# Attention scores of paired heads: from 64 contracted rows to all 128, with each head's keys in a half-zero tile

## The reference, cut to what matters

```python
# ret, 5 heads, chunks of 128 tokens
intra = jnp.einsum('bnihd,bnjhd->bnhij', qc, kc).astype(f32) * decay_in
# moba, 5 heads
s_own = (jnp.einsum('bhqd,bhkd->bhqk', qc, k_own).astype(f32) * scale
         - slopes[:, None, None] * (q_pos[:, None] - own_pos[None, :]).astype(f32))
# mla, 6 heads, 64 + 32 dimensions
s = (jnp.einsum('bqhd,bkhd->bhqk', qn, k_nope)
     + jnp.einsum('bqhd,bkd->bhqk', qp, k_pe)).astype(jnp.float32) * scale
# dilated, 8 heads
scores = jnp.einsum('bnqrhe,bnkrhe->bnrhqk', qb.astype(F32), kb.astype(F32)) * (e ** -0.5)
```

## Time and profile before

| | |
|---|---|
| time, median of 3 executions | 2071.74 us (2069.88 to 2073.74) |
| the profiled execution, its own time | 2070.45 us |
| its span, first to last instruction | 2068.7 us |
| mean granted TensorE clock | 0.987 of 2.4 GHz |
| PE busy | 2012.9 us (97%), 9640 matmul passes |
| DVE busy, ACT busy | 1511.9 us (73%), 1239.2 us (60%) |
| attention steps of layer 0, of layer 1, dilated | about 50 to 125 us, 378 to 455 us, 1690 to 1746 us |

### The profile page before, as it was taken

One profiled execution on the slowest core, in us unless ns is written; L12 is line 12 of the kernel. 1 busy time (PEld: TensorE's weight loads), 2 busy tenths in 40 slices (PEclk: granted clock), 3 DMA queues, 4 the chain that ended last, 5 costly groups with the idle time before them and its releaser, 6 DMA issues.

```text
span 2068.7 us, 26452 instructions
## 1 busy us (share of the span) xinstructions
PE 2012.9 (97%) x9640; PEld 1677.9 (81%) x9640; DVE 1511.9 (73%) x1530; ACT 1239.2 (60%) x1298; POOL 98.5 (5%) x93
## 2 busy tenths in 40 slices
PE   7999999997999999999999999999899999999998
PEld 6878887886888888888888888878688888898887
DVE  6675446667999999989988998999754556565544
ACT  5544344545777777777777777777544455445443
POOL 0000000001000000000000000060010030000000
PEclk9989999998999999999999999999999999999999
DMA  8337554335999999999999999999655443435550
GB/s 336 119 128 273 182 181 156 133 109 222 380 378 383 376 383 376 381 374 383 380 379 372 383 385 368 370 407 364 220 183 188 161 168 143 163 118 198 183 185 38
DMA packets 78919, 548.73 MB, mean 265 GB/s; under 512 B 9008, under 2 KB 9136, under 8 KB 17280
## 3 DMA queue, kind: packets, MB, share of 16 engines
q1 hardware_dynamic: 73872, 522.98, 67.0%
q0 software_dynamic: 4960, 24.56, 3.2%
HBM read 540.68 MB, written 10.49 MB: 266 GB/s over the span
## 4 chain that ended last, share of the span: by engine, by line
PE 91%; DVE 5%; ACT 2%; issue 1%; DMA 0%; DVEq 0%; SPq 0%; ACTq 0%
PE ps L536 28%; PE ps L538 28%; PE ps L537 28%; DVE wlo L1843 2%; PE ps L812 1%; ACT whi L1386 1%; PE ps L709 1%; PE ps L1100 0%; PE ps L1121 0%; PE ps L1128 0%; PE ps L1002 0%; PE ps L982 0%; DMA bc<-in_rows 0%; DVE r L1923 0%; PE ps L1117 0%
## 5 line engine op out<-in xcount | busy, mean ns | idle before, releaser
L1843 DVE TENSOR_TENSOR wlo<-raw,whi 128x2048 fp32r<-128x2048 f32 (+4 forms) x506 | 1147.3, 2271 | 314.5 <-ACT whi L1386 307.7
L1386 ACT ACTIVATE whi<-raw 128x2048 fp32r<-128x2048 f32 (+4 forms) x506 | 950.4, 1879 | 201.1 <-PE ps L538 192.0
L536 PE MATMUL ps<-whi,xth 128*128 128x512 f32 (+3 forms) x1872 | 746.4, 399 | 8.6 <-DVE xtl L1881 3.8
L538 PE MATMUL ps<-whi,xtl 128*128 128x512 f32 (+3 forms) x1872 | 726.0, 388 | 0.0
L537 PE MATMUL ps<-wlo,xth 128*128 128x512 f32 (+3 forms) x1872 | 724.8, 387 | 0.0
L536 PEld LDWEIGHTS ps<-whi,xth 128*128 128x128 f32 x1872 | 354.8, 190 | 79.7 <-issue 8.0
L538 PEld LDWEIGHTS ps<-whi,xtl 128*128 128x128 f32 x1872 | 354.2, 189 | 70.5
L537 PEld LDWEIGHTS ps<-wlo,xth 128*128 128x128 f32 x1872 | 355.4, 190 | 63.1
L536 PE MATMUL ps<-whi,hth 128*128 128x512 f32 (+2 forms) x736 | 287.3, 390 | 2.1 <-DVE htl L2110 1.0
L538 PE MATMUL ps<-whi,htl 128*128 128x512 f32 (+2 forms) x736 | 285.4, 388 | 0.0
L537 PE MATMUL ps<-wlo,hth 128*128 128x512 f32 (+2 forms) x736 | 284.6, 387 | 0.0
(11 more groups left out here) (344 smaller groups left out, 1258.7 us busy)
## 6 DMA issues: line engine op xcount, KB each, us to landing
raw<-in_stream SPq DMA_DIRECT2D x475, 1024.0 KB, 5.8
raw<-in_stream SPq DMA_DIRECT2D x16, 768.0 KB, 4.3
bc<-in_rows POOLq DMA_DIRECT2D x4, 1024.0 KB, 4.9
slot_rows<-in_blank POOLq DMA_DIRECT2D x7, 512.0 KB, 9.5
kc<-slot_rows POOLq DMA_DIRECT2D x7, 512.0 KB, 7.6
sum_rows<-r POOLq DMA_DIRECT2D x7, 512.0 KB, 5.7
raw<-in_stream SPq DMA_DIRECT2D x4, 832.0 KB, 8.3
raw<-in_stream SPq DMA_DIRECT2D x4, 640.0 KB, 3.8
```

The source lines that it names most:

```text
L536: pe.matmul(o, ah, bh, start=start, stop=False, skip_group_check=True)
L538: return pe.matmul(o, al, bh, start=False, stop=stop, skip_group_check=True)
L1386: act.activation(whi[:, c.split, 0:c.width], raw[:, c.raw, 0:c.width], ACT.Copy).then_inc(hi_done, 1)
L1843: dve.tensor_tensor(wlo[:, c.split, 0:c.width], raw[:, c.raw, 0:c.width], f32(whi[:, c.split, 0:c.width]), ALU.subtract).then_inc(lo_done, 1)
```

## The change

Each head of a pair gets a key tile of its own with all 128 rows. They lie in columns 384 to 511 of `prob` (for the first head of a pair) and `probt` (for the second), 2 x 128 columns each. DVE sets the 64 rows that belong to the other head to zero, once, at the start of the program. ACT's one copy of a pair's queries and keys becomes three: the queries of both heads (128 rows x 256), the first head's keys (64 x 256) and the second head's keys (64 x 256). Since these key tiles have one buffer each and not two, the first key copy waits until the scores of head i-2 are done (semaphore `s` at i-1), the second for those of head i-1. `scores` contracts all 128 rows: the queries of both heads against the keys of one, so the other head's queries meet zeros. `mla` heads are left as they are.

```diff
+        lone_keys = [tile[:, :, 3 * P:4 * P] for tile in (prob, probt)]
...
                 def scores(n):
-                    rows = slice(HD * (n % 2), HD * (n % 2) + HD)
-                    q, k = qkt[rows, n // 2 % 2, 0:S], qkt[rows, n // 2 % 2, S:2 * S]
+                    q, k = qkt[:, n // 2 % 2, 0:S], lone_keys[n % 2]
...
                 def scores(i):
                     kind, n = WORK[i]
                     u = UNIT_OF[i]
-                    rows = slice(0, QD) if kind == "mla" else slice(HD * PAIR_OF[WORK[i]][1], HD * PAIR_OF[WORK[i]][1] + HD)
-                    q, k = qkt[rows, u % 2, 0:S], qkt[rows, u % 2, S:2 * S]
+                    rows = slice(0, QD if kind == "mla" else P)
+                    q, k = qkt[rows, u % 2, 0:S], qkt[rows, u % 2, S:2 * S].rearrange("p (t s) -> p t s", t=T)
+                    if kind != "mla":
+                        k = lone_keys[PAIR_OF[WORK[i]][1]]
                     o = ps[B_S]
                     pe.wait_ge(*at(hd, "qk", u + 1))
                     if i == 0:
                         pe.wait_ge(sem(f"kv{l}"), 1)
+                        pe.wait_ge(sem("blank_keys"), 2)
...
+            def take_pair(stage, i, buf):
+
+                act.activation(qkt[:, buf, 0:S], ps[B_TQ][:, 0:S], ACT.Copy)
+                for slot in range(2):
+                    rows = slice(HD * slot, HD * slot + HD)
+                    if i > 0:
+                        act.wait_ge(*at(stage, "s", i - 1 + slot))
+                    m = act.activation(lone_keys[slot][rows], ps[B_TQ][rows, S:2 * S].rearrange("p (t s) -> p t s", t=T), ACT.Copy)
+                m.then_inc(sem("qk"), 1)
...
-                    act.activation(qkt[:, i // 2 % 2, :], ps[B_TQ][:, :], ACT.Copy).then_inc(sem("qk"), 1)
+                    take_pair("dil", i, i // 2 % 2)
...
-                        d = QD if UNITS[u][0] == "mla" else P
                         act.wait_ge(*at(hd, "tq", u + 1))
-                        act.activation(qkt[0:d, u % 2, :], ps[B_TQ][0:d, :], ACT.Copy).then_inc(sem("qk"), 1)
+                        if UNITS[u][0] == "mla":
+                            act.activation(qkt[0:QD, u % 2, :], ps[B_TQ][0:QD, :], ACT.Copy).then_inc(sem("qk"), 1)
+                        else:
+                            take_pair(hd, i, u % 2)
...
+            for slot in range(2):
+                dve.memset(lone_keys[slot][HD * (1 - slot):HD * (2 - slot)], 0.0).then_inc(sem("blank_keys"), 1)
             layer_norm("emb", 0, lambda t: dve.wait_ge(sem(f"x_in{t}"), 16))
```

More of the change, by code:

```diff
@@ L918, in scores @@
                         pe.wait_ge(sem("ws_t"), 2)
-                    pe.matmul(o[:, 0:P], q[:, 0:P], k[:, 0:P], start=True, stop=True)
+                    pe.matmul(o[:, 0:P], q[:, 0:P], k[:, 0, :], start=True, stop=True)
                     pe.matmul(o[:, P:P + S], q[:, P:S], k, start=True, stop=True).then_inc(sem("s"), 1)
@@ L1116, in scores @@
                     if kind == "ret":
-                        pe.matmul(o[:, 0:S], k[:, 0:P], q, start=True, stop=True)
-                        m = pe.matmul(o[:, S:S + P], k[:, P:S], q[:, P:S], start=True, stop=True)
+                        pe.matmul(o[:, 0:S], k[:, 0, :], q, start=True, stop=True)
+                        m = pe.matmul(o[:, S:S + P], k[:, 1, :], q[:, P:S], start=True, stop=True)
                     else:
-                        pe.matmul(o[:, 0:P], q[:, 0:P], k[:, 0:P], start=True, stop=True)
+                        pe.matmul(o[:, 0:P], q[:, 0:P], k[:, 0, :], start=True, stop=True)
                         m = pe.matmul(o[:, P:P + S], q[:, P:S], k, start=True, stop=True)
```

## The result

| | before | after |
|---|---|---|
| median of 5 executions | 2071.74 us (2069.88 to 2073.74) | 2058.29 us (2056.32 to 2062.07) |
| ratio, 95% interval | | 0.9941 (0.9931 to 0.9952) |
| profiled execution, its span | 2070.45, 2068.7 us | 2059.58, 2057.7 us |
| mean granted clock of that execution | 0.987 | 0.991 |

The sign was right and the size was not.

A forecast was written before the change was run, and what follows sets the result against it. The chain that ended last lay on PE for 91% of the span. Mixers -6.2, dilated rows -0.15 and dilated copies +0.3 gave -6.0 us, a median of 2065.7 us, range 2062.6 to 2069.4.

The forecast's parts named there:

- The loss of a 64-row step: PE's score step of a paired head: 0.39 us lost per head at entry, inside and exit against 96 rows.
- Rival 1: No gain, since the loss belongs to something other than the number of rows: 2071.7 or 2072.0 us; chance 0.07.
- The rule that full rows lose the overlap of weight loads: PE's scores: by the notes, weight loads overlap only across different row groups; 0 instead of 0.39 per head, 2071.7 us.
- The way through the mixers: Each mixer up to the end of the DVE and ACT chain: 2.15 us saved before it, 0 inside it.
- ACT's extra work, the wait at i = 10 and the memsets: ACT and DVE in the mixers: 0.55 us more copying per pair, the wait and the memsets, all covered: 0.
- rival 3: ACT's queue becomes the bound at each pair step and PE waits for exponentials: slower, 2079.4 us; chance 0.05.
- Head 14 ... I take 0.55. Head 15: 0.39: Mixer heads behind the DVE and ACT chain: these savings in us per layer, head 14 in a 1.2 GHz stretch.
- the fixed clock: PE behind the chain: the forecast kept the 6.9 us at 1.2 GHz in layer 0 as they were.
- Rival 2: New waiting doubles the 1.2 GHz stretch behind the chain: 2072.6 us for both layers, 2069.1 for one; chance 0.08.
- I take +0.3 for the stage: Dilated attention: copies delay POOL's gating_norm, which overlaps the second lo more; 0.3 us slower, between 0 and 1.0.
- I take 0.15: Dilated attention: full rows save 0.15 us at head 3's scores, the other heads 0.
- Rival 4: All 8 dilated heads pay as well: 3.1 us less, 2062.6 us; chance 0.06.

The follow-up runs named there:

- experiment 5: Kernel before, with the scores of the twelve `mla` heads cut from 96 contracted rows to 64: median 2073.70 us, ratio 1.0014.
- experiment 6: Changed kernel, with all paired scores contracting rows 0 to 95 instead of 128: median 2062.46 us, ratio 0.9946 to the kernel before.
- experiment 1: Changed kernel with its new copies, waits and key tiles, but all paired scores on 64 rows: median 2069.62 us, ratio 0.9988 to the kernel before.
- Experiment 9: Kernel before, with twelve transposes that compute nothing added per mixer in step 15, where PE waits: median 2067.57 us, ratio 0.9988.
- experiment 7: Changed kernel, with 128 rows only in heads 11 to 15 of both mixers, 64 elsewhere: median 2061.35 us, ratio 0.9961 to the kernel before.
- experiments 7 and 8: Changed kernel, 128 rows only in mixer heads 11 to 15 (2061.35 us, ratio 0.9961), or only in heads 0, 1, 8, 9, 10 (2062.74 us, 0.9968).

## Why the prediction was right and wrong

**The loss of a 64-row step: right, a little too large.** 0.39 where transposes of 128 columns precede the scores, 0.34 where outputs of 64 columns do. Experiments 5 and 6 show the cause that was only inferred from the `mla` heads: the row count, with 64 on one side and 96 and 128 on the other. Rival 1 fell. The rule that full rows lose the overlap of weight loads did not show: scores on 128 rows are spaced like those on 96. TensorEngine Tiling (Array Packing) in the Trainium skill, "Key Properties", has the one that fits: a change of the tiling mode drains the engine. The 0.10 at entry agrees with it and comes back at every `mla` step of experiment 5.

**The way through the mixers: right.** 1.9 us in each layer up to and over the chain on DVE and ACT for 2.15 forecast, nothing of it inside. ACT's extra work, the wait at i = 10 and the memsets cost nothing (experiment 1), so rival 3 fell.

**Behind the chain: the term failed.** "Head 14 ... I take 0.55. Head 15: 0.39" reckoned with the stretch at 1.2 GHz as given. It went from 6.9 us to none in layer 0, where the rest of the mixer gained 3.6 for 0.94, and to 3.4 us in layer 1 (1.6 for 0.94); the stretch behind the dilated attention went as well (1.5 for 0), as it did with the copies alone. Where the stretch stayed, the term was about right: the kernel of experiment 6 has the changed kernel's steps, kept 6.8 us at half clock in layer 0 and gained 1.2 us there. So the step that failed is the fixed clock, and not the price of heads 14 and 15. Rival 2 had the right object and the wrong sign: it held that more waiting ahead of the stretch lengthens it. Experiment 9 shows that idle time there takes part in setting it off. But idle time alone does not decide: with waits of 0.69, 1.14 and 0.69 us, all longer than before or as long, the changed kernel had no stretch in layer 0 and 3.4 us in layer 1, and the tail kernel of experiment 7 had 3.4 us and none. By the mean clocks of all executions the change takes 51 - 40 = 11 us from the time at half clock, an estimated 2.7 to 4.4 us at 0.24 to 0.4 us each. Why it takes them away rather than adding is open: experiments 7 and 8 find a part with the tail heads alone and a part with those ahead alone. Since a stretch may occur in one execution and not in the next, the profiled executions differ by 11.0 and the medians by 13.4.

**The dilated attention: both terms failed.** "I take +0.3 for the stage": the delay of POOL was seen, but priced as a longer overlap, a second lo of up to 3.34 us. It changed the order of two instructions 0.2 us apart, the second lo became shorter too (2.41), and the stage gained 1.1 in the profile of experiment 1, whose median is 1.9 lower. "I take 0.15" for the rows: the chain of before was read as if it stayed when its longest piece went; with it gone, PE's steps came back onto the path, and the rows gave 1.3 (2.4 less 1.1). Rival 4's 3.1 was not reached.

The sum with what was found: mixers 2 x (1.9 + 0.94) = 5.7, dilated stage 2.4, clock 2.7 to 4.4: 10.8 to 12.5 us, where the ratio says 12.2 (10 to 14). The 0.94 is still the forecast's and the clock's part an estimate, so the agreement is weak support. The range had no room for it, because the clock was held fixed in every case but the one that made it worse.

## What to carry to other kernels

A pair of matmuls on 64 rows among others on 128 costs 0.34 to 0.39 us in spacing that no duration shows; compare distances between starts with those of a step that differs in one thing, and if half-zero operands are cheap to keep, use all rows. Before pricing a shift of a fraction of a microsecond, look for pairs of instructions that are about to swap, here a DVE pass and a POOL pass 0.18 us apart. And count the stretches at half clock as something that a change to PE's waits can take away or add: filling short waits with matmuls that compute nothing is worth trying in its own right.

## What the runs showed of the hardware that was not expected

- PE's clock fell to 1.2 GHz for 6.9 us among waits of 0.46, 0.80 and 0.69 us, spread over 5 us with work between (0.94 us busy of 2). Twelve transposes of 0.11 us in those waits kept it at 2.4 GHz. With waits of 0.69 and 1.14 us ahead it fell for 6.8 us (experiment 6, layer 0), for 3.4 (the changed kernel, layer 1) or not at all (the changed kernel, layer 0).
- The stretches vary between executions of one kernel: the kernel before took 2067.0 us on average at a mean clock of 0.991 (3 executions) and 2072.0 at 0.987 (17).
- A POOL pass of 1.91 us and a DVE subtraction of 1.76 us, both over SBUF, exclude each other: 3.34 for DVE when it comes second, 3.12 for POOL when it does.
- The same pair of score matmuls has its starts 0.28 us apart behind outputs of 64 columns (L1124 to L1125 above) and 0.23 us behind transposes of 128 columns. It goes with what stands before and not with the rows: the first `mla` head of each layer, on 96 rows behind outputs of 64 columns, has 0.28 too. Why is open.
